# First stage of a two-layer hybrid backbone: order of the first gate's modulation, place of w_mod's unit 5, and a scratch sigmoid before the router

## The reference

```python
ml = modulation(c, w_mod[i], b_mod[i]); mc = modulation(c_ctx, w_mod[i], b_mod[i])
hx = modulate(x, ml[0], ml[1])                 # x * (1 + scale) + shift
yx = pool_mixer(hx, pool_w[j], pool_scale[j], rows)
x = post_norm(x, yx, ml[2], ln_g[i, 0], ln_b[i, 0])      # layer_norm(alpha * x + gate * y)
x = post_norm(x, moe(modulate(x, ml[3], ml[4]), ...), ml[5], ln_g[i, 1], ln_b[i, 1])
```

## Time and profile before

| | us |
|---|---|
| median of 3 runs | 907.65 (904.01 to 908.26) |
| the profiled execution, its own time | 908.33 |
| its span in the profile | 906.5 |
| PE busy | 743.4 |
| DVE busy | 477.1 |
| ACT busy | 316.8 |
| POOL busy | 298.7 |

### The profile page before, as it was taken

The page is one execution under the profiler, slowest core; times in us unless marked ns, Lnnn a source line. Parts: engine busy times, 40 slices in busy tenths (PEclk is TensorE's granted clock), DMA queues, the critical chain, the costliest instruction groups (busy, mean ns, idle before and its releaser), DMA issues. The chain is left out here.

```text
span 906.5 us, 15495 instructions
## 1 busy us (share of the span) xinstructions
PE 743.4 (82%) x5225; PEld 433.2 (48%) x5225; DVE 477.1 (53%) x1089; ACT 316.8 (35%) x776; POOL 298.7 (33%) x702
## 2 busy tenths in 40 slices
PE   0978769999999078999999999999898546999950
PEld 0645335555554013645576665766655233555520
DVE  0038654433334593543767677776754753443326
ACT  0231321222222215644557565575641121222211
POOL 0000112434334100275354746548450012434330
PEclk9999988999999559995999999999997857999985
DMA  9999999999791699475351433513120299999912
GB/s 241 388 382 389 419 408 407 407 409 361 290 407 64 253 389 272 158 248 174 83 146 42 117 90 79 147 42 117 42 59 1 83 403 387 405 405 406 379 66 111
DMA packets 107239, 219.34 MB, mean 242 GB/s; under 512 B 28293, under 2 KB 63437, under 8 KB 102817
## 3 DMA queue, kind: packets, MB, share of 16 engines
q1 hardware_dynamic: 98207, 200.39, 61.6%
q0 software_dynamic: 8224, 15.76, 4.6%
q10 hardware_dynamic: 740, 2.32, 0.9%
HBM read 212.09 MB, written 17.33 MB: 253 GB/s over the span
## 5 line engine op out<-in xcount | busy, mean ns | idle before, releaser
L1232 PE MATMUL banks<-h_cols,weight_ring 128*128 128x512 f32 (+1 forms) x384 | 160.8, 539 | 0.7
L1209 POOL TENSOR_TENSOR arena<-arena 128x60 f32<-128x60 f32 (+24 forms) x248 | 81.9, 330 | 125.0 <-DMA arena<-blocks 106.2
L1211 POOL TENSOR_TENSOR arena<-arena 128x60 f32<-128x60 f32 (+24 forms) x248 | 83.5, 337 | 19.4
L901 POOL DMA_INDIRECT y_of_tokens<-arena,place_now x42 | 46.7, 1111 | 128.8 <-ACT arena L793 128.8
L745 PE MATMUL banks<-arena 128*64 128x512 f32 x352 | 85.2, 605 | 3.0 <-DVE arena L837 3.0
L1232 PEld LDWEIGHTS banks<-h_cols,weight_ring 128*128 128x128 f32 x384 | 66.5, 195 | 34.9 <-issue 31.9
L873 POOL DMA_INDIRECT arena<-h_of_tokens,row_now x50 | 53.0, 1060 | 82.7 <-DVE token_of_slot L713 38.7
L287 PE MATMUL banks<-weight_ring,c_cols 128*32 128x512 f32 x368 | 51.5, 675 | 30.8 <-DMA weight_ring<-in_w_mod_dram 30.8
L763 PE MATMUL banks<-weight_ring,arena 128*64 128x256 f32 x576 | 67.6, 388 | 0.9 <-DVE arena L825 0.9
L829 DVE TENSOR_TENSOR arena<-arena,banks 128x128 f32<-128x128 f32 x42 | 12.1, 287 | 104.2 <-ACT arena L798 99.3
L798 ACT ACTIVATE arena<-banks 128x128 f32<-128x128 f32 x42 | 11.6, 277 | 144.1 <-PE banks L763 121.6
(11 more groups left out here) (290 smaller groups left out, 1377.8 us busy)
## 6 DMA issues: line engine op xcount, KB each, us to landing
weight_ring<-in_w_mod_dram SPq DMA_DIRECT2D x46, 1024.0 KB, 10.0
weight_ring<-in_dn_w_in_dram SPq DMA_DIRECT2D x32, 512.0 KB, 7.1
weight_ring<-in_w_gate_dram SPq DMA_DIRECT2D x13, 1024.0 KB
weight_ring<-in_w_up_dram SPq DMA_DIRECT2D x13, 1024.0 KB
weight_ring<-in_w_down_dram SPq DMA_DIRECT2D x13, 1024.0 KB
arena<-in_w_gate_dram SPq DMA_DIRECT2D x7, 1024.0 KB
arena<-in_w_up_dram SPq DMA_DIRECT2D x7, 1024.0 KB
arena<-in_w_down_dram SPq DMA_DIRECT2D x7, 1024.0 KB
```

Of the source, the lines that this page charges most:

```text
L901: pool.indirect_dma_start(y_halves, bass.IndirectOffsetOnAxis(m.place_now[:, u:u + 1], 0), v.y_tile[u], None, bounds_check=last_row, oob_i ...
L1209: then(pool.tensor_tensor(part, U[:, 0:q, j:j + 1].to_broadcast([P, q, BLK - 1 - j]), M[:, j, j + 1:BLK].unsqueeze(1).to_broadcast([P, q, ...
L1211: ins = pool.tensor_tensor(U[:, 0:q, j + 1:BLK], U[:, 0:q, j + 1:BLK], part, ALU.subtract)
L1232: mm = pe.matmul(bank(6 + j % 2)[:, 0:CTX + SEQ - n0], head_w[h % 2][:, j, k, :], m.hT[:, k, n0:CTX + SEQ], start=(k == 0), stop=(k == KD ...
```

## The change

On PE, the spread of unit 1 moves ahead of pool_y(0). On DVE, `dve_mod(1)` moves from behind the last of the 16 scalings to behind the 12th (c equal to 5), so four scalings come after it. Unit 5's 8 steps are placed anew around the router's products: steps 0 and 1 in `beside`, steps 2 to 4 in `behind`, steps 5 to 7 in a new callback `last`, after the products on L565. `act_router` begins with a sigmoid of `c_rows` into `c_silu`, whose result nobody reads; this holds for both layers.

```diff
-        def pe_router(pe, L, beside=lambda: None, behind=lambda: None):
+        def pe_router(pe, L, beside=lambda: None, behind=lambda: None, last=lambda: None):
@@ end of pe_router, behind the products of L565
             mm.then_inc(s("router_mm"), 1)
+            last()
 
         def act_router(act, L):
             t_ = L.tag
+            act.activation(m.c_silu[:, :], m.c_rows[:, :], ACT.Sigmoid)
             for n in range(2 * L.tiles):
@@ PE's list
             beside([(1, i) for i in range(4)])
+            pe_mod_spread(pe, 1, 0)
             pe_pool_y(pe, 0)
-            pe_mod_spread(pe, 1, 0)
             pe_pool_y(pe, 1)
@@
             def in_router():
                 pe_mod_spread(pe, 4, 0)
-                beside([(5, i) for i in range(5)])
-            pe_router(pe, L0, in_router, lambda: beside([(5, i) for i in range(5, KD)]))
+                beside([(5, i) for i in range(2)])
+            pe_router(pe, L0, in_router, lambda: beside([(5, i) for i in range(2, 5)]), lambda: beside([(5, i) for i in range(5, KD)]))
             pe_mod_spread(pe, 5, 0)
@@ DVE's list
             for c in range(KD):
                 dve_scale(dve, c)
-            dve_mod(dve, 1)
+                if c == KD - 3:
+                    dve_mod(dve, 1)
             dve.wait_ge(s("mod_ready"), READY_END[1])
```

## The result

The changed kernel takes 903.02 us as the median of 18 runs (900.53 to 905.41), the kernel before 907.50 us in 18 runs beside it (903.25 to 910.97). The ratio is 0.995 with a 95% interval of 0.9938 to 0.9962: 3.4 to 5.6 us faster. That is inside the range on record (902.6 to 908.3), but outside the forecast's own part of it (903.6 to 907.0): the middle value is 4.5 us where 2.35 was forecast, and 903.02 is a time that the first rival had named (902.0 to 903.5). The profiled execution took 900.66 us, the second fastest of its 18, with a span of 898.8; the one of before took 908.33.

What follows compares the result with a forecast made beforehand. Layer 0's experts run at PE's pace and start when their first tile can. Gate 0.7, unit 5 0.6, clock 0.9 and layer 1's table 0.15 sum to 2.35 us off 907.65: 905.3 us, range 902.6 to 908.3.

Steps and rivals of the forecast that it cites:

- first rival: Full clock at pool_y(0) and at the router's turns or first expert tile: 902.0 to 903.5 us, chance 0.15.
- The gate: Spread 1 and unit 1's sum earlier: DVE's third sum 0.7 us earlier, bounds 0.2 and 2.1.
- Spread 1 runs on PE at 61.8, in the gap, and takes 1.06 to issue: On PE before pool_y(0): the moved spread fills idle time and takes 1.06 us.
- The table of the sigmoid: Router on ACT: 1.28 us load vanishes, about 0.15 us per layer since PE's products end just after it.
- Unit 5: Layer 0's router: steps placed anew make dve_mod(5) earlier, worth 0.6 us, bounds -2.0 and 2.2.
- is there at 121.05: Load of unit 5's step 7: arrives at 121.05 as DMA is full, needed at 122.7.
- slower rival: Unit 5's last three steps at half clock cost 2.6 us more, 0.9 not had: 908.8 us, chance 0.12.
- The clock of spread 5: Second pair of unit 5's chunks at full clock as PE idles less: 0.9 us, bounds 0 and 0.9.
- worth up to 1.6: First expert tile losing one half-clock stretch, up to 1.6 us, counted only within the faster-clock rival of chance 0.15.

Runs made afterwards that it cites:

- gate alone: The kernel before with only spread 1 moved ahead of pool_y(0) and unit 1's sum behind the twelfth scaling: 907.93 us, ratio 1.0004.
- 2/4/2: The changed kernel with one step of unit 5 moved from behind the table's products to ahead of them: 903.28 us, ratio 0.9941.
- warm tile kernels: The changed kernel with unread products ahead of each layer's first expert tile: 128x512 gave 904.91 us, 128x256 sized to the gap 901.75 us.
- sized warm pool: The changed kernel with 4 unread products (128x384) in PE's gap before spread 1: 900.88 us, ratio 0.9915.
- without gate: The changed kernel with the moves of spread 1 and unit 1's sum undone: 904.08 us, ratio 0.9963.
- sigmoid alone: The kernel before with only the scratch sigmoid added in both layers: 908.13 us, ratio 0.9991.
- 2/6/0: The kernel before with unit 5's steps 2 to 7 between counts and table, none behind the table: 907.28 us, ratio 0.9998.
- unit 5 alone: The kernel before with only unit 5's steps placed anew, 2, 3 and 3: 903.99 us, ratio 0.9967.
- 5/0/3: The kernel before with only unit 5's steps 5 to 7 moved behind the table's products: 908.37 us, ratio 1.001.
- warm pool: The changed kernel with 8 unread products (128x384) ahead of spread 1 and one behind it: 904.68 us, ratio 0.9964.

## Why the prediction was right or wrong

**The gate: 0.7 forecast, nothing measured alone.** The frame was right: PE's chain through pool_y(2) ends last, and much of what the first sum gains is gone at the third. The size was low: with the old gate the third sum stands 26.1 to 27.3 us behind unit 0's (before and five kernels, 26.8 in the mean), with the new one 26.4 in after, 25.1 in gate alone, 25.2 in 2/4/2 and 24.8 in both warm tile kernels, which are as after up to there (25.3 in the mean). That is 1.6 us, within the bounds on record (0.2 to 2.1) and over twice the 0.7. Part of it is the profile that I read: pool_y(0) took 5.29 us in it, and 6.4 to 6.5 in four of the five other kernels with the old gate. Wrong was the step "Spread 1 runs on PE at 61.8, in the gap, and takes 1.06 to issue": it ran at half clock, 2.08 us, in front of pool_y(0) in after and in both warm tile kernels, while in 2/4/2 (1.13) and gate alone (1.26), behind the same gap, it did not. I had counted the half clock for pool_y(0) and not for what I moved ahead of it; the sized warm pool shows that price, 2.6 us against after and 1.0 to 1.4 against the others. Wrong too was that the 0.7 would reach the end by itself: in the old split it ends at step 7, as gate alone shows, and in the new one it reaches unit 5's sum but, in the profiles, not the rows (see without gate).

**The table of the sigmoid: 0.15 per layer.** Right by the traces: 0.16 in layer 0 (1.26 to 1.10), and in layer 1 from the start of L542 to the sigmoid 1.07 against 1.26, 0.2. The time alone could not have told. The drain of 1.38 us behind a load that the Trainium skill's page "ScalarE: Activation LUTs" states in its section on what ACT_TABLE_LOAD costs is in no row: the sigmoid started 0.02 us behind the load, and with the load gone it moved by 0.16 us.

**Unit 5: 0.6 forecast, about 3 measured (1.2 to 4.8).** The steps came as worked out: the counts 2 us earlier behind the sigmoid, three steps between the table and the sum, unit 5's sum 1.4 earlier in the two profiles (1.3 forecast with the gate). The step that failed is the one under it: that the profiled execution of before stood for the others. In it step 7, whose load "is there at 121.05", was done 0.6 us ahead of the places at 122.7. The hour of the load did stay within 1 us, as I said (it was waited for until 121.10 in sigmoid alone and 120.06 in gate alone); the hour of the tokens' chain moved more, by up to 3.2 us at unit 0's sum. In the executions of gate alone, sigmoid alone and 2/6/0 the places were ready 1.7, 2.2 and 2.5 us before PE was free of step 7. In the plain old order (sigmoid alone) the sum then stands at 73.9, against 70.8 in unit 5 alone: 3.1 us, not 1.4. The re-placement takes the late steps out of the table's way: the wait for their loads, and the half clock at which they ran behind it (each costs 0.9 us more so). In 2/6/0 it is the half clock and the length of six steps alone, without any wait. I had priced this at nothing because in that one trace step 7 was just not in the way. The slower rival (half clock on the last three steps) did not come in after: they took 2.78 us. The split 5/0/3 shows a part of it (3.58).

**The clock of spread 5: 0.9 forecast, not had in after.** PE idled 0.8 us, as I said, and the second pair still ran at 1.2 GHz (2.55 us). In unit 5 alone it took 1.61, with 0.72 us between the pairs of copies instead of 1.67; so it did in without gate, 5/0/3, 2/4/2 and the sized warm pool, five of fourteen profiles. What decides it is not shown.

**Unforeseen: the first tile.** 5.6 to 5.7 us in the three kernels of the change's split, 7.0 to 7.2 in the five of the other splits on before: 1.4 us of the gain in those profiles. It starts at half clock in all eight, and what differs is when the full clock returns. Windows of PE, of before and then of after, whose tiles start at 135.28 and 131.08:

```profile
140.00:141.00 1.00, 1.00 (x8) 0.50 1.04 393
...
134.00:134.50 0.50, 0.50 (x8) 1.00 1.08 418
```

But 2/4/2 and the sized warm pool have 7.2 and 7.1, the latter with the change's own split, so it is not the split's own; what sets the hour of the clock's return against the tile's start is not shown. I had it in a rival only, as one half-clock stretch "worth up to 1.6". With some 2.6 us at the rows (78.7, 78.7, 81.2, 80.7 and 78.8 against 77.1, 76.9 and 77.0) it makes up 4.0 of the 4.5 us; up to the last L745 of layer 0's experts the same two groups differ by 3.7 us in the mean (239.2 against 235.5 behind unit 0's sum). Behind the experts, the profiles of before and after differ by 2.0 us (614.3 against 612.3 from the start of the last L745 to the end); unit 5 alone has 612.4 and without gate 615.1, and the change touches nothing there but layer 1's 0.2, so this is scatter of the profiled execution.

In sum the forecast of 905.3 was 2.3 too slow, by unit 5's under-sized term and by the first tile, which it left out. Of the two other terms the gate's was too small at the third sum and did not reach the rows in the profiles, and the 0.9 of spread 5 was not had in after. That the time falls beside the first rival's is not that rival come true: its pool_y(0) at full clock did not come (9.34 us for two tiles, 7.14 at full clock), only its shorter first tile did. The Trainium skill's page "TensorE: Matmul & The Clock Gate", section on HAM oscillation, agrees with the trace of after: short bursts between waits ran at 1.2 GHz in spread 1, in steps 2 to 4 and in the second pair of chunks. Other traces show the same bursts at 2.4 GHz: spread 1 in 2/4/2 (1.13 us), the second pair in five kernels (1.61), steps 2 to 4 in the warm pool (2.78).

## What to carry to other kernels

Before costing a wait at nothing because the trace doesn't show it, look at how close the two arrivals are: a step that was done 0.6 us before the result it could hold up in one execution was 1.7 to 2.5 us behind it in three others. Keep work that waits for a load out of the queue position ahead of a product that a long chain hangs on; but move both what is ahead of the chain and what holds it, since here neither alone gave a measurable gain. And work moved into a gap of PE can run at half clock (here in three of five profiles): count that, or try unread products of a measured length in the gap.

## What was not expected of the hardware

A float32 product with a stationary operand of 128 columns costs twice what I had taken from the steps of unit 5: the dummies of 512 columns ran 0.86 us each at 2.4 GHz and 1.7 at 1.2 (4.78 us for three, most of it at half clock), where a step of unit 5, four products of 512 columns in four column groups of 32, takes 0.86 us in all. And with four unread products, 2.85 us of PE's time in a gap, the kernel took 900.88 us in 6 runs, against 903.02 in 18 of the change alone. The two were not run side by side; their ratios to before are 0.9915 and 0.995, with intervals that overlap a little, so a gain of some 2 us or more is likely and not shown. That the clock stays up is shown: spread 1 and the two tiles behind it ran at full clock throughout.
